# Reordering the last pass of an expert block: one item's down products, row copy and scatter ahead of the next item's turns and splits

## The reference

```python
def moe_ffn(xn, w_router, b_router, w_gate_up, b_gate_up, w_down, b_down):
    ...
    def expert_block(args):
        xb, e = args                       # 128 rows of one expert
        gu = xb @ w_gate_up[e] + b_gate_up[e]
        gate = jnp.minimum(gu[:, :D_FF], SWIGLU_LIMIT)
        up = jnp.clip(gu[:, D_FF:], -SWIGLU_LIMIT, SWIGLU_LIMIT)
        hid = (up + 1.0) * gate * jax.nn.sigmoid(SWIGLU_ALPHA * gate)
        return hid @ w_down[e] + b_down[e]
    ...
    out = jnp.zeros((Tn, D), xn.dtype).at[tok_sorted].add(y_sorted * w_sorted[:, None])

def reference(x, ..., norm_final_g):
    ...
        h = h + moe_ffn(rms_norm(h, norm_ffn_g[l]), ...)
    return rms_norm(h, norm_final_g)
```

## Time and profile before

| | us |
|---|---|
| median of 3 runs | 1824.86 (1824.43 to 1825.22) |
| profiled execution, its own time | 1825.08 |
| its span in the trace | 1823.3 |
| PE busy | 1789.1 (98% of the span) |
| DVE busy | 1452.3 (80%) |
| ACT busy | 1100.8 (60%) |
| POOL busy | 714.2 (39%) |

### The profile page before, as it was taken

One profiled execution on the slowest core, in us unless ns is written; L12 is line 12 of the kernel. 1 busy time (PEld: TensorE's weight loads), 2 busy tenths in 40 slices (PEclk: granted clock), 3 DMA queues, 4 the chain that ended last, 5 costly groups with the idle time before them and its releaser, 6 DMA issues.

```text
span 1823.3 us, 23880 instructions
## 1 busy us (share of the span) xinstructions
PE 1789.1 (98%) x8584; PEld 1492.8 (82%) x8584; DVE 1452.3 (80%) x1073; ACT 1100.8 (60%) x900; POOL 714.2 (39%) x392
## 2 busy tenths in 40 slices
PE   8999999999999998999999999999999999999996
PEld 6888888897888887888888888888888888888885
DVE  4336667674334689999999999999999999999996
ACT  4223563343332356777777777777777777777774
POOL 1000112420000015654664565466456446646644
PEclk9999999999999999999999999999999999999999
DMA  5223424004442658999999999999999999999995
GB/s 186 94 93 107 171 73 137 18 9 183 149 129 93 231 202 321 379 372 389 375 376 378 377 379 373 385 377 369 380 379 377 373 385 372 378 380 377 377 369 184
DMA packets 126912, 503.90 MB, mean 276 GB/s; under 512 B 25192, under 2 KB 25400, under 8 KB 93780
## 3 DMA queue, kind: packets, MB, share of 16 engines
q1 hardware_dynamic: 114400, 478.57, 68.4%
q0 software_dynamic: 10128, 24.40, 5.7%
q10 hardware_dynamic: 2340, 0.33, 0.1%
HBM read 485.66 MB, written 26.26 MB: 281 GB/s over the span
## 4 chain that ended last, share of the span: by engine, by line
PE 92%; DVE 4%; ACT 2%; DMA 1%; issue 1%; POOL 0%; POOLq 0%; SPq 0%; DVEq 0%; ACTq 0%
PE PB L2375 12%; PE PB L2376 12%; PE PB L2378 12%; PE PB L2282 11%; PE PB L2395 6%; PE PB L2392 6%; PE PB L2393 6%; PE PB L1967 4%; PE PB L1968 4%; PE PB L1969 4%; PE PB L2100 2%; PE PB L2347 2%; PE PB L2355 2%; PE PB L2341 1%; PE PB L2247 1%; DVE acc L1439 1%
## 5 line engine op out<-in xcount | busy, mean ns | idle before, releaser
L523 DVE TENSOR_TENSOR mlo<-mraw,mhi 128x2048 fp32r<-128x2048 f32 x384 | 908.2, 2403 | 51.4 <-ACT mhi L519 51.3
L519 ACT ACTIVATE mhi<-mraw 128x2048 fp32r<-128x2048 f32 x384 | 718.7, 1913 | 107.5 <-PE PB L2378 103.6
L2375 PE MATMUL PB<-mhi,xgT_hi 128*128 128x512 f32 x1012 | 397.4, 393 | 2.7 <-DVE mlo L523 1.6
L2376 PE MATMUL PB<-mlo,xgT_hi 128*128 128x512 f32 x1012 | 394.5, 390 | 0.0
L2378 PE MATMUL PB<-mhi,xgT_lo 128*128 128x512 f32 x1012 | 270.7, 389 | 0.0
L893 POOL TENSOR_TENSOR glu<-glu 128x1024 f32<-128x1024 f32 x32 | 80.9, 2527 | 455.4 <-DVE glu L1853 455.4
L2375 PEld LDWEIGHTS PB<-mhi,xgT_hi 128*128 128x128 f32 x1012 | 190.0, 188 | 43.1 <-DVE mlo L523 2.4
L2378 PEld LDWEIGHTS PB<-mhi,xgT_lo 128*128 128x128 f32 x1012 | 189.9, 188 | 39.9
L2376 PEld LDWEIGHTS PB<-mlo,xgT_hi 128*128 128x128 f32 x1012 | 190.1, 188 | 38.9
L2392 PE MATMUL PB<-mhi,hT_hi 128*128 128x512 f32 x496 | 195.9, 395 | 0.0
L2393 PE MATMUL PB<-mlo,hT_hi 128*128 128x512 f32 x496 | 193.2, 389 | 0.0
(11 more groups left out here) (371 smaller groups left out, 2764.5 us busy)
## 6 DMA issues: line engine op xcount, KB each, us to landing
mraw<-in_w_gate_up_dram SPq DMA_DIRECT2D x256, 1024.0 KB, 9.3
mraw<-in_w_down_dram SPq DMA_DIRECT2D x128, 1024.0 KB, 7.1
raw<-in_w_in_dram SPq DMA_DIRECT2D x27, 1024.0 KB, 4.9
qkvT<-in_w_in_dram SPq DMA_DIRECT2D x8, 1024.0 KB, 4.9
qkvT<-in_w_o_gdn_dram SPq DMA_DIRECT2D x4, 1024.0 KB, 5.0
qkvT<-in_w_o_sconv_dram SPq DMA_DIRECT2D x4, 1024.0 KB, 5.0
qkvT<-in_w_mix_out_dram SPq DMA_DIRECT2D x4, 1024.0 KB, 4.9
qkvT<-in_x_dram SPq DMA_DIRECT2D x4, 512.0 KB, 5.1
```

The costliest lines, as they stand in the source:

```text
L519: nc.scalar.activation(mhi[split_slot(m)][:], mraw[:, raw_slot(m), :], ACT.Copy).then_inc(e_h, 1)
L523: nc.vector.tensor_tensor(mlo[split_slot(m)][:], mraw[:, raw_slot(m), :], mhi[split_slot(m)][:].bitcast(F32), ALU.subtract).then_inc(e_l, 1)
L2375: pe.matmul(gate_up_bank[:, n, :], xgT_hi[:, k, :], w_hi[:, n, :], start=False, stop=False)
L2376: pe.matmul(gate_up_bank[:, n, :], xgT_hi[:, k, :], w_lo[:, n, :], start=False, stop=False)
```

## The change

In the last pass only: PE does chunks 8 to 11 of item `last-1` with `turn_mixing` alone between them (after chunk 10), and only then `turn_hidden(last)` and `bias_product(0)`. ACT does `y_copy(last-1)` ahead of the hi part of the last item's hidden rows. That hi part and DVE's lo part are each made in two halves (`HALVES`), and PE's `last_down` waits for the first half before chunk L0 and for the second before L2. DVE makes the lo part of L2 ahead of these halves. POOL's `scatter` is cut into `aim` (the copies) and `add_rows` (the DMAs), and for item `last-1` the idle step comes ahead of the wait for `y_copy`, which has a semaphore of its own, `s_before_last`. SP issues the load of `final_gain` right after the last weights.

```diff
+        HALVES = (slice(0, GT), slice(GT, KD))
@@ SP
+                    sp.wait_ge(s_mixw, TOPK)
+                    sp.dma_start(final_gain[:], norm_final_g.partition_broadcast(P)).then_inc(s_fg, 16)
                     sp.wait_ge(s_stored, 1)
-                    sp.dma_start(final_gain[:], norm_final_g.partition_broadcast(P)).then_inc(s_fg, 16)
                     for t in range(TT):
                         sp.dma_start(h_rows[:, t, :], sums_by_token[:, t, :]).then_inc(s_back[t], 16)
@@ POOL
                     hidden(last)
-                    scatter(last - 1)
+                    aim(last - 1)
+                    step()
+                    pool.wait_ge(s_before_last, 1)
+                    add_rows(last - 1)
                     pool.sem_inc(s_stored, 1)
@@ ACT
+                    def last_hidden_hi():
+                        act.wait_ge(s_th, last + 1)
+                        for ks in HALVES:
+                            nc.scalar.activation(xgT_hi[:, ks, :], turn_bank[:, ks, :], ACT.Copy).then_inc(s_hh, 1)
...
                     weights_hi(act, last - 1, 12)
+                    weights_hi(act, last - 1, 13)
                     act.wait_ge(s_mixT, 1)
                     nc.scalar.activation(mix_wT[:], ...).then_inc(s_mixc, 1)
-                    weights_hi(act, last - 1, 13)
-                    hidden_hi(last, xgT_hi)
                     weights_hi(act, last, 2)
-                    y_copy(last - 1)
+                    y_copy(last - 1, s_before_last)
+                    last_hidden_hi()
                     weights_hi(act, last, 3)
@@ DVE
+                    def last_hidden_lo():
+                        for n, ks in enumerate(HALVES):
+                            dve.wait_ge(s_hh, last + 1 + n)
+                            nc.vector.tensor_tensor(xgT_lo[:, ks, :], turn_bank[:, ks, :], xgT_hi[:, ks, :].bitcast(F32),
+                                                    ALU.subtract).then_inc(s_hl, 1)
...
                     for m in range(11, 14):
                         weights_lo(dve, last - 1, m)
-                    hidden_lo(last, xgT_lo, xgT_hi)
                     weights_lo(dve, last, 2)
+                    last_hidden_lo()
                     weights_lo(dve, last, 3)
@@ PE
                     def last_down(after):
-                        pe.wait_ge(s_hl, last + 1)
                         for d in range(4):
+                            if d % 2 == 0:
+                                pe.wait_ge(s_hl, last + 1 + d // 2)
                             down_chunk(last, d, d, last_bank, xgT_hi, xgT_lo)
...
                     def second_bias():
-                        pe.wait_ge(s_y, last + 1)
+                        pe.wait_ge(s_before_last, 1)
                         bias_product(1)
 
                     gate_up(last, 0)
-                    down(last - 1, {0: turn_mixing, 1: lambda: bias_product(0), 2: lambda: turn_hidden(last)})
+                    down(last - 1, {2: turn_mixing})
+                    turn_hidden(last)
+                    bias_product(0)
                     last_down({1: second_bias, 2: lambda: bias_product(2)})
```

More of the change, by code:

```diff
@@ L893, in hidden, with aim @@
                         nc.gpsimd.tensor_tensor(hid, up, sig, ALU.mult).then_inc(s_hid, 1)
-                    def scatter(i):
+                    def aim(i):
                         nc.gpsimd.tensor_copy(now[:, 1:2], index[:, bass.ds(i, 1)]).then_inc(s_goal, 1)
@@ L900, in scatter, with add_rows @@
                         pool.wait_ge(s_wrow, i + 2)
-                        pool.wait_ge(s_y, i + 2)
-                        step()
+                    def add_rows(i):
                         nc.gpsimd.indirect_dma_start(sum_d, bass.IndirectOffsetOnAxis(ap=now[:, 1:2], axis=0), y_rows[:], None,
@@ L947, in mix_and_experts @@
                         gather(i + 3)
-                        scatter(i)
+                        aim(i)
+                        pool.wait_ge(s_y, i + 2)
+                        step()
+                        add_rows(i)
                     pool.wait_ge(s_th, last)
                     hidden(last)
-                    scatter(last - 1)
+                    aim(last - 1)
+                    step()
+                    pool.wait_ge(s_before_last, 1)
+                    add_rows(last - 1)
                     pool.sem_inc(s_stored, 1)
@@ L1283, in sigmoid, with hidden_hi, y_copy @@
                         nc.scalar.activation(sig, gate, ACT.Sigmoid, scale=ALPHA).then_inc(s_sig, 1)
-                    def hidden_hi(i, to=hT_hi):
+                    def hidden_hi(i):
                         act.wait_ge(s_th, i + 1)
-                        nc.scalar.activation(to[:], turn_bank, ACT.Copy).then_inc(s_hh, 1)
-                    def y_copy(i):
+                        nc.scalar.activation(hT_hi[:], turn_bank, ACT.Copy).then_inc(s_hh, 1)
+                    def last_hidden_hi():
+                        act.wait_ge(s_th, last + 1)
+                        for ks in HALVES:
+                            nc.scalar.activation(xgT_hi[:, ks, :], turn_bank[:, ks, :], ACT.Copy).then_inc(s_hh, 1)
+                    def y_copy(i, done=s_y):
                         act.wait_ge(e_used, chunk_number(i, 11) + 1 + SPL)
@@ L1294, in y_copy @@
                         nc.scalar.activation(y_rows[:].rearrange("p (b c) -> p b c", b=2), y_bank, ACT.Copy,
-                                             scale=slot_weight).then_inc(s_y, 1)
+                                             scale=slot_weight).then_inc(done, 1)
                     first_tokens_hi()
@@ L1854, in gated, with hidden_lo @@
                                                        op1=ALU.mult).then_inc(s_prod, 1)
[L1856 removed]
+                    def hidden_lo(i):
                         dve.wait_ge(s_hh, i + 1)
[L1858 removed]
+                        nc.vector.tensor_tensor(hT_lo[:], turn_bank, hT_hi[:].bitcast(F32), ALU.subtract).then_inc(s_hl, 1)
+                    def last_hidden_lo():
[3 more added lines that the diff above has]
+                                                    ALU.subtract).then_inc(s_hl, 1)
                     for m in range(11, 13):
```

1 line of the change is left out of this document (added).

## The result

The changed kernel takes 1827.87 us (median of 20 runs, 1827.01 to 1828.79) against 1824.94 before (20 runs, 1824.28 to 1826.79): 2.9 us more, ratio 1.0016, 95% interval 1.001 to 1.0022. The difference is less than the 0.2% that the prediction took as its limit, but with so many runs it is clear of noise: the change makes the kernel slower. The time lies inside the stated range, beside rival 1's 1828.0 and not at the forecast 1825.5.

A forecast was written before the change was run, and what follows sets the result against it. Tail bound by row copy, scatter and loading sums back, PE's path 1.16 us behind. Loads 2.8 us earlier lie unused; PE 1.65 later delays the first add 0.56, the end 0.6: 1824.86 + 0.6 = 1825.5, range 1824.4 to 1828.0.

The forecast's parts named there:

- rival 1: Clock falls in PE's 4.5 us gap before its last products, costing 2.5 us: 1828.0; chance 0.28.
- PE's slack of 1.16: In the tail, PE's path has 1.16 us of slack against the load path; load-path gains are worth at most this.
- the scatter's gain: Scatter path, with final_gain out of the way, brings the sums 2.8 us earlier (1.5 to 3.5), unused behind PE.
- PE's last products 1.65 later: DVE's lo part of L2 ahead of hidden_lo makes PE start its last products 1.65 us later, at 1794.6.
- The scatter 1.15 earlier: POOL's idle step waits behind DVE's lo part of L2, so the scatter starts at 1794.1, not 1795.25.
- The clock: Forecast case (0.58) had no fall in PE's gap; the rival case (0.28) had a fall to half clock, costing 2.5 us.
- the 5.04 at the kernel's start: Dense transposes taking 5.04 us at half clock; taken as the recovery time after a fall, half of it lost.
- The norm's end: First add 0.56 us later, and POOL's small ops colliding with DVE's finish ops: 0.6 us delay at the end (0.15 to 1.2).

The follow-up runs named there:

- x4: Kernel before with only the load of final_gain moved early, behind the last weights: 1824.12 us, 0.60 under before.
- x1: Changed kernel with DVE's order swapped back, hidden rows' lo halves ahead of the lo part of L2: 1824.26 us, 0.46 under before.
- x2: Kernel before with only DVE's order changed, lo part of L2 ahead of hidden_lo in one piece: 1828.56 us, 3.84 over before.
- x5a: Changed kernel with the last norm's sums kept in PSUM, nothing else: 1826.38 us, 1.44 over before.
- x3: Changed kernel with 16 extra products filling PE's gap ahead of its last products: 1825.81 us, 1.09 over before.
- x6: Changed kernel with DVE's order swapped back and 8 extra products in what is left of PE's gap: 1823.69 us, ratio 0.9993.
- x9: Kernel before with final_gain loaded early and the norm's sums kept in PSUM: 1823.32 us, 1.37 under before.
- x8: Kernel before with the norm's sums kept in PSUM, nothing else: 1824.44 us, 0.25 under before.
- x10: Change with hidden rows' splits ahead of y_copy on ACT and L1's lo part on DVE, norm's sums in PSUM: 1821.59 us, 3.10 under before.

## Why the prediction came out as it did

- **PE's slack of 1.16 decides, and the scatter's gain lies unused: right.** The first add is released by PE. x4 shows the same slack from the other side: an estimated 1.66 us freed on the load path moved the first add by 1.07. The sums' loads were issued at 1801.27 (1800.40), even 2 us earlier than I had put them, and it changed nothing.
- **PE's last products 1.65 later, through DVE's order: right.** 1794.61 against the forecast 1794.6; x1, which takes the order back, and x2, which makes it alone, show that the order is the cause.
- **The scatter 1.15 earlier: right in its start** (1794.96, 1794.09 on the scale of before), wrong behind it: I left its preparation on POOL as it was, 3.61, and it took 1.65.
- **The clock: the wrong case was called the likeliest.** The prediction gave the fall 0.28 and priced it at 2.5. It fell in the profiled executions of the change, of x2 and of x5a, and all 20 runs of the change lie over 1827, where x3, with the same delay and the clock held, has 1825.5 to 1826.4. The step that failed in the choice between the two cases is the sentence that 4.5 us "leaves little beyond" the 3.9 us after which the clock fell at the kernel's end. I read 3.9 as the length that a gap must have. It was one sample of how late the fall can come after work stops; the clock also fell behind x2's 3.69 and x6's 1.95, which were shorter. The Trainium skill, "TensorE: Matmul & The Clock Gate", section "Why this matters for your kernels", advises against idle gaps between bursts of matmuls, as the prediction said. The gaps of 4.34 and 3.69 agree with it; that the clock fell behind 1.76 to 1.95 in other traces goes further than the page does. The price was too high: some 3.4 us at half clock, 1.6 lost in the trace (3.2 later at the end, less 1.64 at the start) and 1.84 by x3, not 2.5, since this recovery was shorter than the 5.04 at the kernel's start. That those 5.04 were at half clock rests on the spacing of the transposes alone: the earlier trace rows give a granted clock of 1.00 for both stretches, as the trace's record of the clock begins only at 12.9.
- **The norm's end: right mechanism, wrong size.** The first add is 0.57 late in x3. I let 0.6 come out at the end and set 1.2 as the bound; 1.24 came out. One more collision was drawn, as the bound had it. x5a puts the whole of POOL and DVE meeting there at 1.5 us in the change.
- **Sum:** 0.6 forecast; 1.09 with the clock held (x3); 1.84 for the clock; 2.93 measured. The range held the time, by 0.13, only because rival 1 was let into it, and not by the forecast. That the total lies so near rival 1's 1828.0 is luck: two errors cancel, 0.5 too little for the norm and 0.7 too much for the clock.

## What to carry to other kernels

Moving work off the bounding path helps only by the slack of the path beside it, so read that slack first and then check what the new order does to it: here 1.16 us of slack stood against a lo part of 2.2 us put ahead of the one op that PE waited for. A gap on PE can cost more than its length where PE is on the bounding path: here the clock fell behind gaps from 1.76 us up, though not behind all of them. Count such a gap ahead of dense products as a risk, and if it can't be closed, fill it. Where DVE and POOL work side by side in a tail, look whether an operand of DVE can come from PSUM.

## What the runs showed of the hardware

- The clock fell behind gaps of 4.34 (the change), 4.35 (x5a) and 3.69 us (x2) in the last pass, and behind 1.95 (x6), 1.88 (x9) and 1.76 (x8) in the routing stage. It held behind one of 2.15 (x1) in the last pass and, in the routing stage, behind one of 1.96 in before and one of 2.75 in the change. So the gap's length alone does not tell. In x2 it fell when PE had been at work for a microsecond. PE in order of time, the change:

```profile
687.30 0.87 PE L2361 MATMUL PB<-ident,xg 128*128 128x128 f32 x6 [2.75 <-DMA xg<-xn_scratch,index]
```

- This gap, 0.8 longer than the one of before, is also most of the 0.87 by which this execution arrived late at the last pass. Nothing that the change moves runs before the last pass, so this is scatter between executions.
- In the change and in x2 the clock was back at 1.00 within some 3.4 us of dense products; in x6, where PE's work had short breaks, it took 6.8.
- POOL's indirect DMA for the scatter took 3.61 in before and 1.65 in the change and x1. In before it began while DVE ran a subtraction of two SBUF operands, in the two others while DVE's operand came from PSUM. x10 lies between: it began under a subtraction too, when 1.2 of it were left, and took 2.73, 1.1 more than 1.65. In before 2.1 were left and it took 2.0 more. That its preparation waits for the end of such a subtraction is the reading that fits all of these; no run took it alone. POOL and DVE in order of time, before:

```profile
1795.25 3.61 POOL L903 DMA_INDIRECT token_sums_scratch<-y_rows,now  x1 [0.17 <-issue]
1795.04 2.29 DVE L523 TENSOR_TENSOR mlo<-mraw,mhi 128x2048 fp32r<-128x2048 f32 x1
```

The same in x10:

```profile
1792.56 2.73 POOL L906 DMA_INDIRECT token_sums_scratch<-y_rows,now  x1 [2.77 <-ACT y_rows L1308]
1791.49 2.28 DVE L523 TENSOR_TENSOR mlo<-mraw,mhi 128x2048 fp32r<-128x2048 f32 x1
```
